# One of the four operand builds of a coefficient group moves from VectorE to GpSimd

## The reference, cut to what matters

```python
s_half, i_half = lax.top_k(s, 16)                      # per head, per half key
top_s, pos = lax.top_k(cand_s, 16)
ids = jnp.take_along_axis(cand_i, pos, axis=-1)        # id = i * 128 + j
gates = jax.nn.softmax(top_s, axis=-1)
a = gelu(einsum('chkd,cd->chk', u_tab[ids], x))
y = einsum('chk,chkd->cd', gates * a, v_tab[ids])
```

## Time and profile before

| what | value |
|---|---|
| median of three runs | 3477.5 us (3471.12 to 3483.51) |
| the profiled execution's own time | 3496.24 us |
| its span in the profile | 3494.4 us |
| TensorE matmul busy | 3328.6 us (95%) |
| VectorE busy | 2984.3 us (85%) |
| ScalarE busy | 2191.8 us (63%) |
| GpSimd busy | 1330.3 us (38%) |

### The profile page before, as it was taken

How to read it: one execution, slowest core, us unless ns; L and a number is a source line. 1 busy time by engine, 2 the same in 40 slices (tenths; PEclk the granted TensorE clock), 3 DMA queues, 4 the chain that set the end, 5 groups by cost and what they waited for, 6 DMA issues and landing times.

```text
span 3494.4 us, 63120 instructions
## 1 busy us (share of the span) xinstructions
PE 3328.6 (95%) x19278; PEld 2443.3 (70%) x19278; DVE 2984.3 (85%) x6039; ACT 2191.8 (63%) x3118; POOL 1330.3 (38%) x1126
## 2 busy tenths in 40 slices
PE   6999999999999999999989999999999998999999
PEld 5767775667777667767777677666677776676776
DVE  6899777998888778888869997789988886888888
ACT  3574435567777666777746724455677776766776
POOL 0000017316555556557500000271265564555554
PEclk9999999999999999999999999999999999999999
DMA  5312272459999999999923123535699999999998
GB/s 199 103 61 69 89 264 97 156 190 326 363 354 331 319 353 345 363 350 359 339 81 90 61 79 121 211 115 179 221 335 361 345 341 310 360 355 351 344 361 296
DMA packets 421669, 868.89 MB, mean 249 GB/s; under 512 B 167824, under 2 KB 233360, under 8 KB 421008
## 3 DMA queue, kind: packets, MB, share of 16 engines
q1 hardware_dynamic: 310512, 544.87, 46.3%
q0 software_dynamic: 73728, 268.47, 21.3%
q10 hardware_dynamic: 37152, 52.45, 4.1%
HBM read 774.41 MB, written 85.98 MB: 246 GB/s over the span
## 4 chain that ended last, share of the span: by engine, by line
PE 40%; issue 26%; DVE 15%; POOL 10%; DMA 4%; ACT 3%; DVEq 0%; POOLq 0%; SPq 0%; ACTq 0%
PE ps L924 9%; PE ps L927 8%; PE ps L928 8%; POOL gbuf L586 6%; POOL spare L600 5%; PE ps L636 4%; PE ps L638 3%; PE ps L637 3%; DVE yT L1506 3%; DVE i L1752 2%; DMA raw<-stream 2%; DVE v L1748 1%; DVE S_ring L1758 1%; DMA gbuf<-u_rows,ids_u 1%; PE ps L670 1%
## 5 line engine op out<-in xcount | busy, mean ns | idle before, releaser
L670 PE MATMUL ps<-h,w 128*128 128x384 f16 (+1 forms) x2272 | 760.0, 335 | 40.1 <-ACT w L1012 40.0
L671 PE MATMUL ps<-h,w 128*128 128x384 f16 (+1 forms) x2272 | 756.8, 334 | 0.0
L1012 ACT ACTIVATE w<-w_hi 128x1024 f16<-128x1024 f32 x544 | 572.5, 1052 | 286.3 <-DVE w L1934 174.5
L600 POOL TENSOR_TENSOR spare<-spare 128x1 f32<-128x1 f32 x504 | 393.9, 782 | 909.2 <-DVE a_sp L1740 500.9
L927 PE MATMUL ps<-cf,w 128*128 128x384 f16 x2032 | 665.2, 328 | 0.0
L928 PE MATMUL ps<-cf,w 128*128 128x384 f16 x2032 | 662.2, 327 | 0.0
L667 PE MATMUL ps<-h_hi,w_hi 128*128 128x384 f32 (+1 forms) x2272 | 489.9, 357 | 0.0
L924 PE MATMUL ps<-cf_hi,w_hi 128*128 128x384 f32 x2032 | 430.6, 354 | 23.6 <-DVE cf L1928 23.6
L1934 DVE SCALAR_TENSOR_TENSOR w<-raw,w_hi 128x1024 f16<-128x1024 f32 x256 | 313.3, 1224 | 132.8 <-ACT w_hi L1007 113.6
L667 PEld LDWEIGHTS ps<-h_hi,w_hi 128*128 128x128 f32 x2272 | 396.0, 189 | 17.4 <-issue 0.3
L1000 ACT ACTIVATE w_hi<-raw 128x1024 fp32r<-128x1024 f32 x296 | 313.7, 1060 | 144.6 <-DMA raw<-stream 105.5
(11 more groups left out here) (286 smaller groups left out, 6241.7 us busy)
## 6 DMA issues: line engine op xcount, KB each, us to landing
raw<-stream SPq DMA_DIRECT2D x682, 512.0 KB, 5.6
gelu_scratch<-g_out ACTq DMA_DIRECT2D x256, 192.0 KB, 6.0
cg<-gelu_scratch SPq DMA_DIRECT2D x256, 192.0 KB, 6.8
c_scratch<-stage SPq DMA_DIRECT2D x128, 256.0 KB
cg<-c_scratch SPq DMA_DIRECT2D x256, 128.0 KB, 5.7
qT<-ada SPq DMA_DIRECT2D x32, 512.0 KB, 6.2
cgate<-ada SPq DMA_DIRECT2D x32, 512.0 KB, 5.4
w_rows<-ada SPq DMA_DIRECT2D x32, 512.0 KB, 6.4
```

Of the source, the lines that this page charges most:

```text
L600: nc.gpsimd.tensor_tensor(spare[:, 16:17], spare[:, 17:18], spare[:, 18:19], ALU.add).then_inc(room, 1)
L670: nc.tensor.matmul(ps[:, b, 0:n], w16[:, s, 0, c], h16[:, c, 1, t0:T], start=False, stop=False)
L671: mm = nc.tensor.matmul(ps[:, b, 0:n], w16[:, s, 1, c], h16[:, c, 0, t0:T], start=False, stop=c == C - 1)
L1012: nc.scalar.mul(w16[:, s, 1], w_hi[:, s].bitcast(F32), X_DOWN).then_inc(w16_done, 1)
```

## The change

The product of `one_j` and the gate's remainder, `gated_lo`, is computed by GpSimd in place of VectorE. On GpSimd it waits for `j_done` and signals a new semaphore, `gated_low_done`, for which TensorE's `c_group` waits besides `lr_done`. VectorE's `gated_hi` now carries `lr_done`. GpSimd's gathers, until now one loop, are distributed over the groups: after `gated_low(g)` come the gathers that replace the rows of the group's dot products, up to `dots_by(g + 1) + SLOTS`.

```diff
+                def next_gather(n):
+                    pool.wait_ge(room, l * (2 * P - SLOTS) + n - SLOTS + 1)
+                    pool.wait_ge(row_used, l * 2 * P + n + 1)
+                    nc.gpsimd.tensor_tensor(spare[:, 16:17], spare[:, 17:18], spare[:, 18:19], ALU.add).then_inc(room, 1)
+                    gather(n)
+                def gated_low(g):
+                    pool.wait_ge(j_done, l * GROUPS + g + 1)
+                    nc.gpsimd.tensor_tensor(gated_lo[:, g % 2], one_j[:, g % 2], spread_out(gate_lo, g),
+                                            ALU.mult).then_inc(gated_low_done, 1)
...
-                for n in range(SLOTS, 2 * P):
-                    pool.wait_ge(room, l * (2 * P - SLOTS) + n - SLOTS + 1)
-                    pool.wait_ge(row_used, l * 2 * P + n + 1)
-                    nc.gpsimd.tensor_tensor(spare[:, 16:17], spare[:, 17:18], spare[:, 18:19], ALU.add).then_inc(room, 1)
-                    gather(n)
+                gathers = SLOTS
+                while gathers < DOTS_FIRST + SLOTS:
+                    next_gather(gathers)
+                    gathers += 1
+                for g in range(GROUPS):
+                    gated_low(g)
+                    while gathers < dots_by(g + 1) + SLOTS:
+                        next_gather(gathers)
+                        gathers += 1
+                for n in range(gathers, 2 * P):
+                    next_gather(n)
...
                     pe.wait_ge(lr_done, l * GROUPS + g + 1)
+                    pe.wait_ge(gated_low_done, l * GROUPS + g + 1)
...
-                    nc.vector.tensor_tensor(gated_hi[:, g % 2], one_j[:, g % 2], spread_out(gate_hi, g), ALU.mult)
-                    nc.vector.tensor_tensor(gated_lo[:, g % 2], one_j[:, g % 2], spread_out(gate_lo, g),
+                    nc.vector.tensor_tensor(gated_hi[:, g % 2], one_j[:, g % 2], spread_out(gate_hi, g),
                                             ALU.mult).then_inc(lr_done, 1)
```

More of the change, by code:

```diff
@@ L421, in build_trunk @@
         j_done = sem("j_done")
+        gated_low_done = sem("gated_low_done")
         h_tr = sem("h_tr")
@@ L431, in build_trunk, with spread_out @@
         y_tr = sem("y_tr")
+        cube = [P, GROUP // 2, NKEYS, 2]
+        def spread_out(x, g):
+            return x[:, GROUP * g:GROUP * (g + 1)].rearrange("k (a o b) -> k a o b", o=1, b=2).broadcast_to(cube)
         v_rows = stream.rearrange("n p c q -> (n p) (c q)")
@@ L1883, in _ @@
                 dve.wait_ge(rt_ev, (l + 1) * NBD)
-                cube = [P, GROUP // 2, NKEYS, 2]
-                def spread_out(x, g):
-                    return x[:, GROUP * g:GROUP * (g + 1)].rearrange("k (a o b) -> k a o b", o=1, b=2).broadcast_to(cube)
                 for g in range(GROUPS):
```

## The result

The changed kernel takes 3572.3 us in the median of four runs (3570.63 to 3574.3), the kernel before 3479.5 us in four: ratio 1.027, interval 1.0249 to 1.0291. The change costs 93 us. The profiled execution has a span of 3569.0 us, 74.5 us more than before; the rest of the difference is that the profiled execution of before was slower than its median.

The account below looks back on a forecast made before the run. TensorE, loads and VectorE were taken as nearly full in the group stretches. VectorE's 424 us plus 31 idle gave +51 us a layer, +102 on 3496.2, so 3598; against the median 3580 us, range 3510 to 3650.

Parts of the forecast that it names:

- What bounds the stretch: In the two coefficient-group stretches, TensorE, loads and VectorE are all nearly full; a lighter VectorE returns some 12 us a layer.
- The relief: In the group stretches, VectorE loses 33 us of busy time a layer; at most some 12 us can come back.
- The hold: In each group, GpSimd's reading keeps out VectorE's `gated_hi` or a dot product; the operands are ready some 1.7 us later.
- The product's length: `gated_low` on GpSimd takes 2.36 us a group, lower bound 1.9, upper 2.98; 113 us a layer.
- What idle remains: VectorE's remaining waits in a stretch: 10 us for loads (high parts) and 21 us for gathered rows, 31 a layer.
- The sum: Per layer, VectorE's 343.5 - 33 + 113 = 424 us plus 31 idle makes 455, +51; two layers +102 us.
- The second way: GpSimd's 347 us a layer plus waits of 91 and 19 us for VectorE's instructions make 457 us.
- The operands' lateness: At TensorE's `c_group`, both operands come 1.75 us later, against room of 0.13 and 1.46 us in two groups.
- first rival: GpSimd becomes the bound in the group stretches, gathers fall behind, waits for rows grow: 3640 to 3690 us; chance 0.12.
- GpSimd as the bound: In the group stretches, 2.98 us an instruction adds 30 us a layer to the 457: 3640 to 3690 us; chance 0.12.
- The stretch swallows it: Loads truly bound the group stretches, the instruction takes 1.9 us or less: 3475 to 3500 us; chance 0.07.
- The relief arrives: GpSimd's instruction takes about 1.2 us including its wait, so up to 12 us a layer return: 3453 us; chance 0.06.

Follow-up runs that it names:

- the copy: Changed kernel with GpSimd's product replaced by a one-column addition that takes the wait and a one-input copy of `one_j` to `gated_lo`: 3537.7 us, ratio 1.0158.
- the kernel without TensorE's wait: Changed kernel with GpSimd's product written to a scratch tile; TensorE doesn't wait for it and multiplies `gated_hi` twice: 3531.7 us, ratio 1.0135.
- the half product: Changed kernel with the product split, planes 0 and 1 on VectorE, 2 and 3 on GpSimd: 3542.4 us, ratio 1.0163.

## Why the prediction was right

**What bounds the stretch** held. The relief was put at 12 us a layer at most; measured, by leaving the product out, it is 15 us over both.

**The hold** held in mechanism: between two instructions of VectorE, at the next end, for the product's full length, on `gated_hi` or on a dot. Fills in place of the product took away 2.3 of 2.7%. In the Trainium skill, "SBUF — State Buffer", section "Who interferes with whom", a VectorE instruction with two SBUF inputs is said to contend with a GpSimd instruction that reads SBUF and not with one that only writes it. The trace agrees: the product holds `gated_hi` for 1.69 us, the copy holds a dot and a low part for 0.97 and 0.82 us, and under the fills `gated_hi` stays at 0.685 us.

**The product's length** was mis-sized. I took L562's 2.36 us with a lower bound of 1.9. It reads for 1.75 us (906.91 to 908.66 above); its row lasts 1.9 us at the least and 2.05 us in the median with its waiting. The nearest row was L559, the one with a repeated operand, and not L562. The difference is 0.61 us a group, 29 us a layer. Put into the prediction's own line, 343.5 - 33 + 48 x 1.75 = 394.5 us, against 393.6 measured; the window after holds 111 dots where the one before holds 114, which is 3.7 us, so no closer agreement can be read from it. In the Trainium skill, "GPSIMD Engine Reference", section "Elementwise — side-by-side cycle accounting", the rule for two inputs gave an estimated 2.2 us, nearer than L562's row but also too long; this run has 1.75 us for float16.

**What idle remains** was guessed at 31 us; it is 438 - 393.6 = 44.4 us. The parts were the wrong way round: waits for high parts 38.3 us (I kept 10), for rows 3.9 us (I kept 21). The wait for high parts didn't shrink although the loads have room (ScalarE's wait for loads fell from 36.0 to 17.8 us): now ScalarE comes late because TensorE stands at the group's product, which is a wait of the loop and not of the loads. Two rows point the same way. ScalarE's gelu waits 51.2 us for TensorE where it waited 22.1. And in the kernel without TensorE's wait, from 785 to 1180, VectorE's wait for high parts is only 15.2 us.

**The sum** was +102 us against the profiled execution; profile against profile it is +74.5, over by 27. The median forecast, 3580, is nearer to 3572.3 than that, since the profiled execution of before lay 18.7 us above the median of three and that of after doesn't. The closeness of the last figure is in part luck. With 1.75 us for the product and the guessed 31 us of idle, the same sum gives 394.5 + 31 = 425.5 us a layer, and so 3520 us. The product taken too long stood in for what the sum had no term for: a product that stands behind gathers, and the clock that was lower after such waits. The second way, 457 us a layer, was no independent check. It gave GpSimd 347 us of work and 110 us of waiting; measured are 336.8 and 101.2 us, of which 55.0 us are for dots and 29.9 us for `one_j`.

Of the signs named beforehand, the stretches of 438 and 441 us stand at the low end of 440 to 470, and VectorE's 393.6 us and the product's row of 1.9 to 2.27 us are below what was named. The longer `gated_hi` and dots, TensorE's waits at the group's product, ScalarE's shorter waits for loads and the unchanged rest came as said.

**The operands' lateness** was priced as one thing, 1.75 us for both signals. In the change most of TensorE's waiting is for GpSimd's signal (35.0 against 5.4 us), since the product stands behind gathers: TensorE's wait is worth 47 us in all, up to 15 us of them as matmul time at the lower clock, and moving one gather gave 43 us back. The prediction had the product's place ahead of the gathers only as a reason for gathers to be late. That gathers could make the product late it named under its first rival, without a price of its own, and it had no term for TensorE's clock.

**The rivals.** GpSimd as the bound: not here; it waits 30 us for `one_j` and 55 us for dots in a layer. The stretch swallows it: excluded by the half product, which costs 1.6%. The relief arrives: it would need 1.2 us including the wait, and the product takes 1.9 at the least.

## What to carry to other kernels

Moving elementwise work from VectorE to GpSimd is not a transfer from a full engine to an idle one where VectorE's instructions have two SBUF inputs: VectorE gets rid of 0.68 us and is kept out for 1.75 us. Look in the trace for a GpSimd instruction that already overlaps such a one; how much longer than usual the VectorE row is shows the price before anything is built. The wait of the held instruction lies inside its row and not in idle time, so a held engine looks busier. And first leave the instruction out altogether: if that gives only 15 us, moving it elsewhere can hardly give more. Where TensorE gets a new wait, look at its granted clock behind it as well.

## What the runs showed of the hardware that was not expected

A float16 product with one repeated operand reads for 1.75 us on GpSimd. Its shortest row, 1.90 us, is as long as the usual one of L559, whose operands are float32: the narrower type made it no shorter. A hold can be longer than the reading: at 797.41 above, `gated_hi` had the field to itself from 797.49, and the product's row begins only at 797.73, straight behind a gather's; yet `gated_hi` took 2.78 us, that is 2.1 us of hold. It looks as if a part of GpSimd begins the product while its gather still runs. No run tested this. A gather alone doesn't hold VectorE: in the kernel before, the 96 `gated_hi` last between 0.677 and 0.689 us, and in the first stretch 21 of the 48 overlap the issue of a gather.

A gather's issue takes very different times on GpSimd for the same form. In the kernel with one gather behind the product:

```profile
902.19 0.95 POOL L593 DMA_INDIRECT gbuf<-u_rows,ids_u  x1
...
909.41 1.79 POOL L593 DMA_INDIRECT gbuf<-u_rows,ids_u  x1 [0.15 <-POOL spare L601]
```

At 902.19 VectorE is idle (901.77 to 903.34), at 909.41 it runs dots back to back. Whether it is their reading that stretches the issue was not tested by itself.
